# The selected-block values of a decoding step as 64-row matmuls, and a split load of the pages in front of a key/value load

## The reference, cut to what matters

```
kc, vc = compress(past + new)          # one compressed key/value per 16 positions: reads slots 0, 1 of all pages
o_cmp, idx = nsa_compressed(q, kc, vc) # attention over them; idx: the 16 best blocks of 64 positions
k_sel, v_sel = pages[idx], slots 2, 3  # the selected blocks
p = masked_softmax(q @ k_sel)
o_sel = p @ v_sel                      # what the change computes in another shape
o_win = attention over the last 512 positions
out = g0 * o_cmp + g1 * o_sel + g2 * o_win
```

## Time and profile before

| What | Value |
|---|---|
| Median of three runs | 2228.89 us (2227.23 to 2232.06) |
| Time of the profiled execution | 2227.23 us |
| Its span, first to last instruction | 2225.5 us |
| Mean granted TensorE clock | 0.942 of full speed |
| TensorE busy (matmul) | 2027.1 us, 91% |
| VectorE, ScalarE busy | 837.2 us, 697.2 us |
| Read from and written to memory | 280.75 MB, 40.26 MB |

### The profile page before, as it was taken

One profiled execution on the slowest core, in us unless ns is written; L12 is line 12 of the kernel. 1 busy time (PEld: TensorE's weight loads), 2 busy tenths in 40 slices (PEclk: granted clock), 3 DMA queues, 4 the chain that ended last, 5 costly groups with the idle time before them and its releaser, 6 DMA issues. The chain is left out here.

```text
span 2225.5 us, 36741 instructions
## 1 busy us (share of the span) xinstructions
PE 2027.1 (91%) x14465; PEld 1640.4 (74%) x14465; DVE 837.2 (38%) x1664; ACT 697.2 (31%) x1328; POOL 50.6 (2%) x99
## 2 busy tenths in 40 slices
PE   7999999999999799968997698999996699999998
PEld 7999999999999455655554344444443599989998
DVE  6233235423332344526564134334334422242332
ACT  6332223333332222205663223332232321142222
POOL 0000000000000100000000000000000011100000
PEclk9999999999999788858999899999997899999999
DMA  5452233333331433220123758888874642223220
GB/s 190 163 186 78 88 98 98 107 101 107 100 110 52 157 140 140 82 106 29 58 70 139 241 187 290 292 296 319 302 266 152 239 136 76 81 86 107 91 81 22
DMA packets 163710, 315.16 MB, mean 142 GB/s; under 512 B 18893, under 2 KB 68430, under 8 KB 160466
## 3 DMA queue, kind: packets, MB, share of 16 engines
q1 hardware_dynamic: 143656, 278.98, 37.3%
q10 hardware_dynamic: 19882, 33.83, 4.2%
HBM read 280.75 MB, written 40.26 MB: 144 GB/s over the span
## 5 line engine op out<-in xcount | busy, mean ns | idle before, releaser
L250 PE MATMUL mm<-x_hi,w_hi 128*128 128x288 f32 x1696 | 368.7, 299 | 13.5 <-DVE w_lo L381 13.5
L250 PE MATMUL mm<-x_hi,w_lo 128*128 128x288 f32 x1696 | 364.2, 296 | 0.0
L250 PE MATMUL mm<-x_lo,w_hi 128*128 128x288 f32 x1696 | 364.1, 296 | 0.0
L250 PEld LDWEIGHTS mm<-x_hi,w_hi 128*128 128x128 f32 x1696 | 274.7, 189 | 15.1 <-issue 12.3
L381 DVE TENSOR_TENSOR w_lo<-w_raw,w_hi 128x1024 fp32r<-128x1024 f32 x106 | 129.8, 1225 | 385.2 <-ACT w_hi L280 385.2
L250 PEld LDWEIGHTS mm<-x_hi,w_lo 128*128 128x128 f32 x1696 | 274.3, 189 | 0.0
L250 PEld LDWEIGHTS mm<-x_lo,w_hi 128*128 128x128 f32 x1696 | 274.0, 189 | 0.0
L1501 PE MATMUL s_pH<-wide,cw_sample 128*128 128x512 f32 x512 | 243.2, 617 | 22.2 <-DMA wide<-pages 19.7
L1988 PE MATMUL o_mm<-o_feat_hi,o_w_hi 128*128 128x288 f32 x1024 | 225.4, 302 | 24.7 <-DVE o_feat_lo L2063 17.6
L1988 PE MATMUL o_mm<-o_feat_lo,o_w_hi 128*128 128x288 f32 x1024 | 221.4, 298 | 0.0
L1988 PE MATMUL o_mm<-o_feat_hi,o_w_lo 128*128 128x288 f32 x1024 | 221.2, 298 | 0.0
(11 more groups left out here) (404 smaller groups left out, 2283.0 us busy)
## 6 DMA issues: line engine op xcount, KB each, us to landing
wide<-pages SPq DMA_DIRECT2D x256, 256.0 KB, 5.4
w_raw<-w_in SPq DMA_DIRECT2D x106, 512.0 KB, 3.9
s_kv<-pages ACTq DMA_DIRECT2D x128, 256.0 KB, 8.7
s_kv<-pages SPq DMA_DIRECT2D x128, 256.0 KB, 9.0
o_w_raw<-w_out SPq DMA_DIRECT2D x16, 1024.0 KB, 8.0
o_w_raw<-ple_gate SPq DMA_DIRECT2D x16, 1024.0 KB, 7.4
m_state<-state SPq DMA_DIRECT2D x4, 2056.0 KB, 12.7
state_sample<-m_state SPq DMA_DIRECT2D x4, 2056.0 KB, 6.6
```

Of the source, the lines that this page charges most:

```text
L250: last = nc.tensor.matmul(mm[:, s % 3, y, 0:HALF], w[:, m % RING, kk, :], f[:, k, y * HALF:(y + 1) * HALF], start=k == 0 and i == 0, stop= ...
```

## The change

1. **SyncE.** The second half of `wide` is loaded in two calls of 8 pages. The first stands where the whole stood; the second stands behind the first quarter of `s_kv`, and ahead of the third. Both count on the same semaphore.
2. **TensorE.** `values(b, q)` makes 2 matmuls for each page instead of 4: 64 rows of probabilities (two heads) with 128 columns of values (the same two heads), as in the window's values.
3. **VectorE.** The four scalings of 32x64 become one call of `scaled` over 128x128, whose `diag` zeroes the products of one head with the other's values. The clearing of `out[:, 2, :]` at the stage's start goes, since the whole tile is now written.

```diff
@@ -1473,10 +1473,13 @@
                     sp.dma_start(wnd[:], a["win_pages"][b + 1]).then_inc(wnd_in, 16)
                 if b + 2 < NB:
                     sp.wait_ge(h_done, 4 * (b + 1) + 4)
-                    load_comp(sp, b + 2, HP, NPG)
+                    load_comp(sp, b + 2, HP, HP + QP)
                 if b + 1 < NB:
                     sp.wait_ge(pv_done, PARTS * b + 2)
                     load_kv(sp, b + 1, 0)
+                if b + 2 < NB:
+                    load_comp(sp, b + 2, HP + QP, NPG)
+                if b + 1 < NB:
                     sp.wait_ge(pv_done, PARTS * b + 6)
                     load_kv(sp, b + 1, 2)
             sp.wait_ge(out_ready, NB)
@@ -1606,14 +1609,13 @@
                 if q == 0:
                     pe.wait_ge(x_ready, 3 * b + 1)
                 for i in range(4 if q < NQ else 1):
-                    for g in range(KV):
-                        rows, own = slice(32 * g, 32 * g + 32), half(g % 2)
+                    for gp in range(2):
                         if q < NQ:
-                            v0 = 256 + g * AD
-                            last = mm(pO[rows, 0, own], probT[:, q % 2, i, rows], kvp[:, 4 * q + i, v0:v0 + AD],
+                            v0 = 256 + gp * P
+                            last = mm(pO[half(gp), 0, 0:P], probT[:, q % 2, i, half(gp)], kvp[:, 4 * q + i, v0:v0 + P],
                                       start=q == 0 and i == 0, stop=False)
                         else:
-                            last = mm(pO[rows, 0, own], probT[0:TSA, q % 2, 0, rows], B.vsel_new[:, g * AD:(g + 1) * AD],
+                            last = mm(pO[half(gp), 0, 0:P], probT[0:TSA, q % 2, 0, half(gp)], B.vsel_new[:, gp * P:(gp + 1) * P],
                                       start=False, stop=True)
                 last.then_inc(pv_done, 1)
 
@@ -1777,7 +1779,6 @@
             last.then_inc(gate_parts, 1)
             v.memset(imp[:], 0.0)
             v.memset(kcn[:], 0.0)
-            v.memset(out[:, 2, :], 0.0)
             v.memset(pgp[:], 0.0)
             v.memset(diag[:], 0.0)
             v.memset(pick[:], 0.0)
@@ -1871,10 +1872,7 @@
                 step(v.reciprocal(col[:, 1:2], col[:, 1:2]))
                 step(v.tensor_tensor(col[:, 1:2], col[:, 1:2], gcol[:, 1, b:b + 1], ALU.mult))
                 dve.wait_ge(pv_done, PARTS * (b + 1))
-                for g in range(KV):
-                    rows, own = slice(32 * g, 32 * g + 32), half(g % 2)
-                    last = v.tensor_scalar(out[rows, 2, own], pO[rows, 0, own], col[rows, 1:2], None, ALU.mult)
-                last.then_inc(x_ready, 1)
+                scaled(2, 0, col[:, 1:2])
             gathered(NB - 1)
 
         @block.gpsimd
```

## The result

The changed kernel takes 2277.77 us (median; 2277.18 to 2282.7) against 2228.89, 49 us slower. The ratio is 1.0223, with a 95% interval of 1.0204 to 1.0241. The forecast was 2260, with 2273 as the upper end of the range. The direction and the place are as forecast, but the time lies above the range: +49 us, where the prediction's sum was +32.4.

What follows compares the result with a forecast made beforehand. TensorE (busy 91% of the span) and, in this stage, DMA engines (0.83) were near full. Six batches 25.0, old waits -1.1, batch 6 into 7 0.7, batch 7 2.8, clock 5: +32.4 us, so 2260; range 2238 to 2273.

Steps and rivals of the forecast that it cites:

- Values, 0.43 us a chunk and 0.66 a batch: TensorE's values phase: each chunk's matmuls cost 0.43 us more; after idle time absorbs some, the next batch starts 0.66 late.
- old waits: TensorE's waits of 0.72 and 0.42 us where it first reads `wide`'s second half, counted as -1.1 us.
- The six waits: TensorE waits for the last page of `wide` in batches 1 to 6: 3.5 us each, ends 1.4 and 5.0.
- the run of 31 pages: DMA engines, from ScalarE's first page landing (1385.5) to `wide`'s last: 30 intervals of 0.68 us, plus 1.4, so 1407.3.
- The upper bound of 5.0 us: Upper end of each wait for `wide`: one more of ScalarE's pages ahead and the full 2.2 us correction, landing at 1408.8.
- The clock: Lowered clock in full TensorE work behind the six waits: 1.75 us each, bounds 0 and 10.5, half taken: 5 us.
- Batch 7: Last batch: all 3.6 us of added matmul work show, less 0.8 for the single scaling: 2.8 us.
- VectorE, the dropped clearing, `s_kv` early: Scaling 0.82 us less, worth it only at the last gather; dropped clearing worth nothing; earlier first quarter of `s_kv` worth 0.
- (a): Rival: `wide`'s last pages land in time, only the matmuls count: +6.3, about 2235 us; chance 0.10.
- (c): Rival: matmuls cost by the instruction, 18 ns each, a chunk 0.29 us; with pages in time -7, about 2222; chance 0.04.
- (d): Rival: nothing to measure, pages in time and the 0.66 us absorbed: +2 to +4, 2232 us; chance 0.06.
- (b): Rival: waits for `wide` and clock losses at their upper ends: +47, 2276 us; chance 0.08.

Runs made afterwards that it cites:

- e1: The changed kernel with the loads in the old order, so only the values' matmuls, the scaling and the dropped clearing are new: 2230.22 us, ratio 1.0007.
- e5: The changed kernel with 18 filler matmuls on TensorE right before its wait for the second half of `wide`, batches 1 to 6: 2268.05 us, ratio 1.0184.
- e9: e10 with the new values' matmuls in place of the old and without the values phase's filler: 2226.10 us, ratio 0.9987.
- e10: The same kernel as e8, run again on the chip of e9 to compare the two: 2221.82 us, ratio 0.9964.
- e7: The changed kernel with ScalarE's load of the last quarter of `s_kv` moved behind its last copy before the scores: 2294.13 us, ratio 1.0297.
- e6: The kernel before with 5 filler matmuls ahead of chunk 4's transposes: 2226.32 us, ratio 0.9995.
- e8: The kernel before with `wide`'s second half in two calls ahead of `s_kv`, one VectorE scaling, fillers in the values phase and batch 7: 2219.71 us, ratio 0.9965.

## Why the prediction was wrong

- *Values, 0.43 us a chunk and 0.66 a batch.* Right: 1.02 us a chunk, and the values phase is 0.67 longer (15.62 for 14.95). Its cost was over-stated, since the clock that it holds up was priced at nothing: +0.6 us in e1's six batches, where 6 x 0.66 = 4.0 less 1.1 of old waits was forecast.
- *The six waits.* Right in place, number and cause, too small: 5.26, 5.24, 6.25, 4.65, 5.72 and 5.70, together 32.8 for 21. **The failed step is the start of the run of 31 pages.** I put the first landing at 1385.5, 15.0 us after the last compression matmul. In the changed kernel, where that matmul ends at 1379.3 and not 1370.5, it came 16.9 after: issued 0.5 later, and landed 4.0 us after its issue and not 2.6, behind the first 8 pages of `wide`, the last of which lands at 1394.7, only 1.5 us before it. From there the 31 pages took 21.7 us, as forecast (20.4 + 1.4). The 2.6 was misread: in the earlier trace rows it is the landing of the first page of `wide`, which SyncE sent into idle engines, and not of one of ScalarE's pages. ScalarE's pages, issued from 1382 to 1389, had their own figure in the trace before:

```profile
DMA to landing us min/median/max: 5.6/8.2/11.0
```

  With 5.6 the forecast wait would have been 3.0 us longer, 6.5; the measured 4.0 lies between. The upper bound of 5.0 us bounded the filling of the engines and not this start.
- *The clock.* **The second failed step.** I gave it half a chance and 5 us. It fell in every one of the six batches: the busy time behind the waits grew by 10.9 us, and e5 gives back 9.9. That is about 1.8 of the 7.6 us that a batch lost, and a higher chance was in reach: the rows showed a lowered clock behind 2.15 us of idle already.
- *Batch 7.* 4.3 for 2.8 in the changed kernel, 2.1 in e1, with the same instructions. In e1 the values phase alone is 2.8 longer, as forecast. In the changed kernel it is 4.0 longer, because its first transposes and its first chunk of values run at half speed (1.98 us for 16 instructions that take 1.09 later). Why the low stretch lies differently in each was not followed further.
- *VectorE, the dropped clearing, `s_kv` early.* Right: the last gather's wait is 0.52 for 1.36; nobody waits for `s_kv`.
- *The rivals.* (a), (c) and (d) are refuted by the waits and by 64 ns an instruction; (b), all waits and all clocks at their upper ends, named 2276 and came nearest; its wait of 5.0 was still exceeded in five of the six batches.

The sum, from the traces: the waits are +31.7 and everything else in the six batches +13.9, of which 10.9 is the clock in the matmuls behind the waits. The other 3.0 is the compressed scores, also in part at the low clock (4.8 us for 3.9), the values phase (longer, less what its own clock gives back: some 1.2 by e1), and about 0.9 that was not followed. That is +45.6. Batch 7 is +4.3 and the way to batch 1 +2.1, together +52.0. The spans differ by 51.1, so -0.9 lies behind the stage.

The Trainium skill, "TensorEngine Tiling (Array Packing)", Instruction Overhead, as the prediction's estimate reads it, would have had the larger matmuls win. The traces don't bear that out: e9 is behind e10 by 3.5 us in six batches and by 3.6 in batch 7's values phase. And its "DMA: Bandwidth & Descriptors", Issuing engines are not separate DMA queues, is half borne out. The two queues share the engines, as it says (e7). But it calls the issue usually small, and here a page costs SyncE 0.56 us to look up and 0.52 to issue against 0.68 to move.

## What to carry to other kernels

Before a transfer is moved behind another, count everything that will share the engines with it between its issue and the wait for it, on all queues, and compare with the spare time at the wait. A wait of TensorE can cost more than its length where full work follows: here the clock fell during each of the six, and each cost 1.8 us more than it lasted. Price both. And extra work in an idle gap can pay for itself by the clock, as in e5, e6 and e8.

## What was not expected of the hardware

- 48 filler matmuls, 36 of them (8.3 us) in an idle stretch of 11 us ahead of short dependent work, bought some 5 us in one batch (clock 0.77 to 0.96).
- Five fillers in each batch's gap of 2.15 us removed the lowered stretch that four of six batches had (2.6 us).
- A page that lands in 4.6 to 6.2 us when its queue has the engines to itself (e7) takes up to 11.6 us with the other queue's pages between: the two queues' pages land in turn, one of each in 1.36 us.
